# Mixing attention: the high and the low half of a head's values as one stationary tile

## The reference, cut to what matters

```python
z = jnp.einsum("bqhd,bkhd->bhqk", qb, kb) * scale
causal = s_idx < t_idx
log_beta = jax.nn.log_sigmoid(z)
log_fail = jnp.where(causal, log_beta - z, 0.0)
survive = lax.cumsum(log_fail, axis=3, reverse=True) - log_fail
a = jnp.where(causal, jnp.exp(log_beta + survive), 0.0)
o = jnp.einsum("bhqk,bkhd->bqhd", a, vb)
```

## Time and profile before

| | us |
|---|---|
| median of three runs | 2083.61 |
| lowest and highest run | 2078.96, 2084.55 |
| time of the profiled execution | 2086.71 |
| its span on the core | 2085.0 |
| outside the span | 1.7 |
| TensorE busy | 1934.9 (93%) |
| VectorE busy | 1078.7 (52%) |
| ScalarE busy | 854.9 (41%) |
| GpSimd busy | 199.7 (10%) |
| mean granted clock of TensorE, 1 is full | 0.937 |
| mixing stage, start to the end of `values(15)` | about 559 |

### The profile page before, as it was taken

How to read it: one execution, slowest core, us unless ns; L and a number is a source line. 1 busy time by engine, 2 the same in 40 slices (tenths; PEclk the granted TensorE clock), 3 DMA queues, 4 the chain that set the end, 5 groups by cost and what they waited for, 6 DMA issues and landing times. The chain is left out here.

```text
span 2085.0 us, 31580 instructions
## 1 busy us (share of the span) xinstructions
PE 1934.9 (93%) x12232; PEld 1686.0 (81%) x12232; DVE 1078.7 (52%) x1500; ACT 854.9 (41%) x1135; POOL 199.7 (10%) x329
## 2 busy tenths in 40 slices
PE   5999999999899988899999979699979999999996
PEld 5999999999899977799998857476757777778884
DVE  4434444433333324655542247999666776754543
ACT  4645555554422223333332224133346556543331
POOL 0100001000000000000000004777200000000000
PEclk8899999999899989999999989678889999999998
DMA  3121222122222233132233226311211212133331
GB/s 116 61 61 61 72 69 72 56 64 70 61 91 91 91 124 110 58 94 91 91 94 98 91 72 160 59 36 33 58 47 50 81 56 80 55 96 108 120 109 78
DMA packets 64501, 165.93 MB, mean 80 GB/s; under 512 B 21808, under 2 KB 21936, under 8 KB 64304
## 3 DMA queue, kind: packets, MB, share of 16 engines
q1 hardware_dynamic: 64432, 164.98, 25.9%
HBM read 154.20 MB, written 8.39 MB: 78 GB/s over the span
## 5 line engine op out<-in xcount | busy, mean ns | idle before, releaser
L1597 DVE TENSOR_TENSOR WL<-WR,WH 128x1024 fp32r<-128x1024 f32 x271 | 335.7, 1240 | 303.4 <-ACT WH L1169 294.2
L1169 ACT ACTIVATE WH<-WR 128x1024 fp32r<-128x1024 f32 x271 | 284.3, 1053 | 216.0 <-PE J L894 78.9
L702 PE MATMUL J<-XH,WH 128*128 128x264 f32 (+1 forms) x1376 | 295.0, 297 | 18.2 <-DVE XL L1601 18.0
L702 PE MATMUL J<-XL,WH 128*128 128x264 f32 (+1 forms) x1376 | 289.2, 293 | 0.0
L702 PE MATMUL J<-XH,WL 128*128 128x264 f32 (+1 forms) x1376 | 288.6, 292 | 0.0
L702 PEld LDWEIGHTS J<-XH,WH 128*128 128x128 f32 x1376 | 225.8, 199 | 23.6 <-issue 17.1
L702 PEld LDWEIGHTS J<-XL,WH 128*128 128x128 f32 x1376 | 224.3, 198 | 0.0
L702 PEld LDWEIGHTS J<-XH,WL 128*128 128x128 f32 x1376 | 223.4, 198 | 0.0
L2220 POOL TENSOR_SCALAR_AFFINE_SELECT E<-E 128x128 f32<-128x128 f32 (+1 forms) x160 | 45.0, 319 | 502.6 <-DVE E L1648 344.5
L923 PE MATMUL J<-X2H,WH 128*128 128x512 f32 x168 | 69.8, 416 | 8.8 <-DVE X2L L1878 8.8
L2242 POOL TENSOR_TENSOR SM<-SM 128x32 f32<-128x32 f32 x15 | 4.6, 309 | 728.3 <-DVEq L1912 727.2
(11 more groups left out here) (417 smaller groups left out, 4472.3 us busy)
## 6 DMA issues: line engine op xcount, KB each, us to landing
WR<-weights SPq DMA_DIRECT2D x271, 512.0 KB, 3.5
X<-tokens SPq DMA_DIRECT2D x4, 528.0 KB, 5.3
H<-tokens SPq DMA_DIRECT2D x1, 2112.0 KB, 8.2
res_dram<-H SPq DMA_DIRECT2D x1, 2048.0 KB, 8.1
u_dram<-UT SPq DMA_DIRECT2D x8, 256.0 KB, 2.2
US<-u_dram SPq DMA_DIRECT2D x16, 128.0 KB, 6.0
gate_dram<-GST SPq DMA_DIRECT2D x8, 256.0 KB, 2.2
GSB<-gate_dram SPq DMA_DIRECT2D x8, 256.0 KB, 3.6
```

The costliest lines, as they stand in the source:

```text
L702: mm = pe.matmul(o[:, 512 * h:512 * h + half], ws[:, s, w], xs[:, a:a + half], start=(k == 0 and i == 0), stop=(k == 7 and i == 2))
L1169: act.activation(WH[:, n % SPLIT, :], WR[:, n % RAW, :], ACT.Copy).then_inc(w_hi, 1)
L1597: dve.tensor_tensor(WL[:, n % SPLIT, :], WR[:, n % RAW, :], WH[:, n % SPLIT, :].bitcast(F32), ALU.subtract).then_inc(w_lo, 1)
```

## The change

The two tiles `VH` and `VL` become one, `VW`, with 64 high and 64 low columns of one head side by side. The stationary tile of a piece is now high | low of head h, 128 columns in all. Two passes, with `AH` and with `AL`, give the product with the high half in partitions 0 to 63 of the PSUM buffer and that with the low half in 64 to 127, the term of both low parts included. The two halves then have to be added: ScalarE copies the lower half (partitions 64 to 127) to a new tile `OT` in SBUF, VectorE adds the upper half to it there, and then ScalarE makes `OH` out of `OT` and VectorE `OL`. The PSUM buffer is freed after the addition.

Below stand the matmuls; then ScalarE's functions, its place in `mix` and its first copy of V; then VectorE's functions and first low part of V.

```diff
-                    for vs, ps in ((VH, AH), (VH, AL), (VL, AH)):
-                        mm = pe.matmul(o[:, at + a:at + b], vs[:, kt * P:(kt + 1) * P], ps[:, c + a:c + b],
+                    for ps in (AH, AL):
+                        mm = pe.matmul(o[:, at + a:at + b], VW[:, kt, h % 2].rearrange("p x d -> p (x d)"), ps[:, c + a:c + b],
...
+                act.wait_ge(o_sum, val(h + 1))
+                act.activation(OH[r, cols(m * L1, L1)], OT[r], ACT.Copy).then_inc(o_hi, 1)
+
+            def head_part(h, t):
...
                 act.wait_ge(pv_done, val(h + 1))
-                act.activation(halves(OH[r, cols(m * L1, L1)]), JV[as_lin(t) % 2][r], ACT.Copy).then_inc(o_hi, 1)
+                if positive(h):
+                    act.wait_ge(o_lo, val(h))
+                act.activation(halves(OT[r]), JV[as_lin(t) % 2][64:P], ACT.Copy).then_inc(o_part, 1)
...
                 if later:
-                    head_out(h - 1, m - 1, t + 2)
+                    head_part(h - 1, t + 2)
                 softplus(h)
                 split_hi(n + 5)
                 fail_hi(h)
+                if later:
+                    head_out(h - 1, m - 1, t + 2)
...
+                head_part(h, t + 9)
+                split_hi(n + 9)
                 head_out(h, m, t + 9)
-                split_hi(n + 9)
                 split_hi(n + 10)
...
-                act.activation(VH[:, 0:3 * P], J[(t + 5) % 2][:, 0:3 * P], ACT.Copy).then_inc(v_hi, 1)
+                act.activation(VW[:, 0:3, :, 0], heads(J[(t + 5) % 2][:, 0:3 * P]), ACT.Copy).then_inc(v_hi, 1)
...
-            def head_out(h, m, t):
+            def head_sum(h, t):
                 h, t = as_lin(h), as_lin(t)
                 r = slice(64 * (h % 2), 64 * (h % 2) + 64)
+                dve.wait_ge(o_part, val(h + 1))
+                dve.tensor_tensor(halves(OT[r]), JV[t % 2][0:64], halves(OT[r]), ALU.add).then_inc(o_sum, 1)
+                dve.wait_ge(o_sum, val(h + 1))
+                dve.nop().then_inc(read_out[t % 2], 1)
+
+            def head_lo(h, m):
...
                 dve.wait_ge(o_hi, val(h + 1))
-                low(halves(OL[r, cols(m * L1, L1)]), JV[t % 2][r], halves(OH[r, cols(m * L1, L1)]))\
-                    .then_inc(read_out[t % 2], 1)
+                low(OL[r, cols(m * L1, L1)], OT[r], OH[r, cols(m * L1, L1)]).then_inc(o_lo, 1)
...
-                low(VL[:, 0:3 * P], J[(t + 5) % 2][:, 0:3 * P], VH[:, 0:3 * P]).then_inc(read_out[(t + 5) % 2], 1)
+                low(VW[:, 0:3, :, 1], heads(J[(t + 5) % 2][:, 0:3 * P]), VW[:, 0:3, :, 0]).then_inc(read_out[(t + 5) % 2], 1)
```

More of the change, by code:

```diff
@@ L194, in halves, with heads @@
     return ap.rearrange("p (h t) -> p h t", h=2)
+def heads(ap):
+    return ap.rearrange("p (k x d) -> p k x d", x=2, d=64)
 def build(nc, weights, cond, params, tokens, bmat, cmat, positions, out):
@@ L236, in build @@
         QL = sb("QL", [P, L1], A1 + 2112, F32R)
-        VH = sb("VH", [P, 5 * P], A1 + 4224, F32R)
-        VL = sb("VL", [P, 5 * P], A1 + 6784, F32R)
+        VW = sb("VW", [P, 5, 2, 2, 64], A1 + 4224, F32R)
         assert A1 + 9344 <= U[8]
@@ L292, in build @@
         GST = sb("GST", [P, S2], M3 + 160)
-        assert M3 + 160 + 2048 <= 212800
+        OT = sb("OT", [P, L1], M3 + 160)
+        assert M3 + 160 + 2112 <= 212800
         M2H, M2L = tile2("M2H", 2), tile2("M2L", 5)
@@ L441, in build @@
         pv_done = sem("pv_done")
+        o_part = sem("o_part")
+        o_sum = sem("o_sum")
         o_hi = sem("o_hi")
+        o_lo = sem("o_lo")
         vt_done = sem("vt_done")
@@ L1244, in head_out @@
                 r = slice(64 * (h % 2), 64 * (h % 2) + 64)
+                act.wait_ge(o_sum, val(h + 1))
+                act.activation(OH[r, cols(m * L1, L1)], OT[r], ACT.Copy).then_inc(o_hi, 1)
+            def head_part(h, t):
+                h = as_lin(h)
+                r = slice(64 * (h % 2), 64 * (h % 2) + 64)
                 act.wait_ge(pv_done, val(h + 1))
-                act.activation(halves(OH[r, cols(m * L1, L1)]), JV[as_lin(t) % 2][r], ACT.Copy).then_inc(o_hi, 1)
+                if positive(h):
+                    act.wait_ge(o_lo, val(h))
+                act.activation(halves(OT[r]), JV[as_lin(t) % 2][64:P], ACT.Copy).then_inc(o_part, 1)
             def mix(m):
@@ L1275, in mix @@
                     act.wait_ge(pv_done, val(h))
-                act.activation(VH[:, 0:3 * P], J[(t + 5) % 2][:, 0:3 * P], ACT.Copy).then_inc(v_hi, 1)
+                act.activation(VW[:, 0:3, :, 0], heads(J[(t + 5) % 2][:, 0:3 * P]), ACT.Copy).then_inc(v_hi, 1)
                 weight_exp(h)
                 act.wait_ge(vt_done, val(2 * m + 2))
-                act.activation(VH[:, 3 * P:4 * P], J[(t + 6) % 2][:, 0:P], ACT.Copy)
-                act.activation(VH[0:META, 4 * P:], J[(t + 6) % 2][0:META, P:2 * P], ACT.Copy).then_inc(v_hi, 1)
+                act.activation(VW[:, 3:4, :, 0], heads(J[(t + 6) % 2][:, 0:P]), ACT.Copy)
+                act.activation(VW[0:META, 4:5, :, 0], heads(J[(t + 6) % 2][0:META, P:2 * P]), ACT.Copy).then_inc(v_hi, 1)
                 weight_hi(h)
@@ L1295, in _ @@
             repeat(act, DT, 1, mix)
+            head_part(HEADS - 1, T_MIX + 10 * DT)
             head_out(HEADS - 1, DT - 1, T_MIX + 10 * DT)
@@ L1604, in _ @@
             dve.memset(PP[:, 0:2], 0.0).then_inc(zeroed, 1)
-            dve.memset(VH[:, 4 * P:].bitcast(F32), 0.0)
-            dve.memset(VL[:, 4 * P:].bitcast(F32), 0.0).then_inc(zeroed, 1)
+            dve.memset(VW[:, 4].bitcast(F32), 0.0).then_inc(zeroed, 1)
             dve.wait_ge(w_hi, 1)
@@ L1678, in mix @@
                 if later:
-                    head_out(h - 1, m - 1, t + 2)
+                    head_sum(h - 1, t + 2)
                 else:
@@ L1684, in mix @@
                 fail_lo(h)
+                if later:
+                    head_lo(h - 1, m - 1)
                 split_lo(n + 6)
                 dve.wait_ge(v_hi, val(2 * m + 1))
-                low(VL[:, 0:3 * P], J[(t + 5) % 2][:, 0:3 * P], VH[:, 0:3 * P]).then_inc(read_out[(t + 5) % 2], 1)
+                low(VW[:, 0:3, :, 1], heads(J[(t + 5) % 2][:, 0:3 * P]), VW[:, 0:3, :, 0]).then_inc(read_out[(t + 5) % 2], 1)
                 dve.wait_ge(v_hi, val(2 * m + 2))
-                low(VL[:, 3 * P:4 * P], J[(t + 6) % 2][:, 0:P], VH[:, 3 * P:4 * P])
-                low(VL[0:META, 4 * P:], J[(t + 6) % 2][0:META, P:2 * P], VH[0:META, 4 * P:])\
+                low(VW[:, 3:4, :, 1], heads(J[(t + 6) % 2][:, 0:P]), VW[:, 3:4, :, 0])
+                low(VW[0:META, 4:5, :, 1], heads(J[(t + 6) % 2][0:META, P:2 * P]), VW[0:META, 4:5, :, 0])\
                     .then_inc(read_out[(t + 6) % 2], 1)
@@ L1709, in mix @@
                 low(YL[:, cols(m * L1, L1)], CT[:], YH[:, cols(m * L1, L1)]).then_inc(y_lo, 1)
-                head_out(h, m, t + 9)
+                head_sum(h, t + 9)
                 split_lo(n + 9)
@@ L1715, in mix @@
                 dve.tensor_copy(MROW[0:2, 0:2 * P], ZT[0:2, 0:2 * P]).then_inc(mod_rows, 1)
+                head_lo(h, m)
                 split_lo(n + 10)
@@ L1734, in _ @@
             repeat(dve, DT, 1, mix)
-            head_out(HEADS - 1, DT - 1, T_MIX + 10 * DT)
+            head_sum(HEADS - 1, T_MIX + 10 * DT)
+            head_lo(HEADS - 1, DT - 1)
             def gates(m):
```

## The result

| | before | changed |
|---|---|---|
| median of 8 runs, us | 2084.61 | 2092.49 |
| lowest and highest, us | 2075.17, 2091.17 | 2091.73, 2094.07 |
| profiled execution, span, us | 2085.0 | 2090.1 |
| mean granted clock | 0.937 | 0.934 |

The changed kernel is slower: the ratio of its runs to those of before is 1.004, 95% interval 1.0021 to 1.006. It does 144 matmuls less. A second series on another chip gave 1.0067 (1.0049 to 1.0085).

What follows compares the result with a forecast made beforehand. TensorE was taken to bound the mixing stage, busy 527 of 561 us. Matmuls gain 10.5 us, copies cost 0, the clock loses 18.6: +8.1 on the median of 2083.6, given as 2091; range 2072 to 2104.

Steps and rivals of the forecast that it cites:

- The matmuls: Values calls of the mixing stage: leaving out nine third passes saves 1.03 us a call; 10.5 us gained in all.
- The call behind the loop: Last values call, after the loop, at 1.2 GHz: a third of its 5.86 us is saved, taken as 2.0 us.
- An iteration at full clock: Loop iteration wholly at 2.4 GHz: 60.8 us forecast; more than 61 us would mean the copies are on the path.
- First heads gain nothing: Eight first-head values calls: in six iterations nothing is gained, as TensorE's wait for `LL` grows from 0.70 to 1.73 us.
- The two calls with cover behind them: First-head values calls in two iterations where TensorE came late itself: 0.68 us each to gain, 1.3 us together.
- The copies cost nothing: Added ScalarE and VectorE steps per head stand where those engines wait: 0 us taken, 20.8 us at most.
- The clock: Mixing loop: one more stretch at 1.2 GHz in each of seven iterations, 2.65 us each, 18.6 us lost.
- The nearest row: First iteration: TensorE idle 1.53 us, then scores; within 1.3 us the clock was at 1.2 GHz, for 6.8 us.
- thin parts nearer together: Second reason for more slow stretches: the same accumulates and scores, with fewer columns between; no size of its own.
- the rule from the Trainium skill: Names long waits for data as what costs the clock; by it a 1.7 us wait before accumulates costs nothing.
- The gain arrives: Rival: the clock falls as often as now, so the 10.5 us are gained: 2073 us, chance 0.30.
- The longer chain: Rival: added copies delay `LL` or `VT` in the mixing stage, 20.8 us at most: 2094 us, chance 0.05.

Runs made afterwards that it cites:

- the moved and filled one: Changed kernel with the second head's scores moved forward and 6 more matmuls at the head of the ada products: 2062.6 us, ratio 0.9893 against the kernel before.

## Why the prediction came out right, and which steps of it did not

**The matmuls: right.** 1.03 us a call was forecast, and 3.08 - 2.03 = 1.05 measured. The call behind the loop took 561.26 to 565.18, 3.92 us, where 5.86 less a third is 3.9.

```profile
561.26 0.56 PE L810 MATMUL J<-AH,VW 128*128 128x264 f32 x1 [4.99 <-DVE AL L1621]
...
565.18 0.51 PE L710 MATMUL J<-XH,WH 128*128 128x258 f32 x1
```

An iteration at full clock was forecast at 60.8 us. The first one of the loop took 62.57, with one stretch of 3.41 us at half clock and the first 0.7 us of another, which is 60.5 without them.

**First heads gain nothing: right.** 1.73 us of wait forecast, 1.77 measured. The two calls with cover behind them, worth 1.3 us, can't be found again, since in the changed kernel other iterations are the slow ones (one wait there is 0.25 us).

**The copies cost nothing: right, and closer than it looks.** The groups over the whole mixing stage, as rows 9 (busy us, mean ns, idle before):

```profile
L1684 DVE TENSOR_TENSOR OT<-J,OT 64x528 f32<-64x528 f32 x16 | 11.2, 697 | 14.7 <-ACT OT L1262 14.7
L1621 DVE TENSOR_TENSOR OL<-OT,OH 64x528 f32 x14 | 9.7, 696 | 0.2
L1262 ACT ACTIVATE OT<-J 64x528 f32<-64x528 f32 x16 | 9.7, 607 | 16.7 <-PE J L810 16.5
L1254 ACT ACTIVATE OH<-OT 64x528 f32 x14 | 9.0, 644 | 6.6 <-DVE OT L1684 6.5
```

The durations are those of the nearest rows to 0.05 us. The strided writes have none either: ScalarE's copy of 128x384 took 486 ns, 489 before. `VT` did come late, as rows 7 let one fear:

```profile
254.22 1.66 DVE L1621 TENSOR_TENSOR LL<-E,LH 128x1440 fp32r<-128x1440 f32 x1 [2.51 <-ACT LH L1234]
...
254.88 0.61 ACT L1285 ACTIVATE VT<-J 128x528 f32<-128x528 f32 x1
...
255.63 0.52 PE L821 MATMUL J<-IDENT,VT 128*128 128x128 f32 x3 [0.41 <-ACT VT L1285]
...
255.93 0.50 PE L791 MATMUL Z<-LH,NTRI 128*128 128x512 f32 x1
```

TensorE waited 0.41 us for it in three iterations, but `LL` ended at 255.88, so the accumulate could not have begun before 255.9 anyway. One wait has taken the place of another. The kernel without the copies agrees with it, against the first series of the changed kernel.

**The clock: the right term, with number and length mis-sized.** Forecast: seven more stretches, sixteen in all, near 80 us. Measured in the profiled execution: four more, thirteen in all, 81.5 us, each longer on average (6.3 in place of 4.8). By the forecast's own reckoning the loop lost 457.4 - 7 x 60.8 = 31.8 us to them, 2.4 us each, and 14.8 us more than before (17.0). 18.6 was forecast. So the net of the loop is +7.6 us, where it was forecast as -7.2 - 1.3 + 18.6 = +10.1. The term had the right sign and came within 4 us, with fewer and longer stretches than it was made of. That the median (2092.5) lies within 2 us of the forecast is in part luck: the second series of the same kernel has a ratio of 1.0067, some 14 us above the kernel before in place of 8.

**The reason given for the clock: half right.** The nearest row, the wait of 1.53 us in the first iteration, was the right one to go by. The second reason, thin parts nearer together, is refuted for second heads by the kernel that shortens these alone; for first heads it was not tried apart from the wait. And the rule from the Trainium skill (TensorE: Matmul & The Clock Gate, section "HAM oscillation — how this bites in real kernels"), by which a wait of 1.7 us would cost nothing, is not borne out here: the kernels with the wait of 1.8 us and those with it filled differ by 24 to 28 us, and the clock fell behind 23 of 38 such waits.

**The rivals.** The gain arrives (2073): this rival needed that the longer wait changes nothing, and that is wrong. Its number is reached, by 2069 to 2070, only when the wait is filled. The longer chain (2094) gave nearly the measured time by a wrong cause; the kernel without copies tells the two apart.

## What to carry to other kernels

Ask of every matmul that goes what TensorE waits for next. If that wait then grows in front of thin matmuls, as here from 0.7 to 1.8 us, the clock can take more than the matmuls gave. The cure is to start the chain that is waited for earlier, or even to fill the wait. Test the two sides of a symmetric change (here first and second heads) apart, since their sum hides that one gains 15 us and the other loses 11.

## What the runs showed of the hardware

- Between 0.9 and 1.8 us of idle time ahead of an accumulate the clock's cost goes from nothing measurable to 24 to 28 us over eight such waits. In the loop of the changed kernel the stretches at 1.2 GHz do not only become more. Some begin earlier, inside the thin matmuls, and last 13.7 us or more, in place of at most 6.8.
- Stretches at 1.2 GHz also come where TensorE did not wait. The kernel with 15 matmuls in the wait has ten of them in the loop, though in its profile it never waits there for `LL`.
- The spread of the runs differs much between kernels, and between series of one kernel: 2091.7 to 2094.1 and 2091.3 to 2102.6 for the two series of the changed kernel, 2086.7 to 2112.7 for the one that shortens first heads alone, 2059.2 to 2063.3 for the moved and filled one. What sets it was not tried.
- GpSimd's five masks take 1.18 us or 2.10 us. In the kernel with the moved scores they take 2.10, beside VectorE's split of weights, which starts just ahead of them; by these rows the 0.9 us between the two durations are more than the 0.65 us of wait that was left. In the changed kernel, at the same step, they take 1.18. That VectorE slows GpSimd here is inferred from the two rows and was not tried by itself.

With the scores moved:

```profile
268.95 1.66 DVE L1669 SCALAR_TENSOR_TENSOR E<-Z,E 128x1440 f32<-128x1440 f32 x1
270.52 1.22 DVE L1619 TENSOR_TENSOR WL<-WR,WH 128x1024 fp32r<-128x1024 f32 x1
270.68 2.10 POOL L2252 TENSOR_SCALAR_AFFINE_SELECT E<-E 128x128 f32<-128x128 f32 x5 [11.62 <-DVE E L1669]
```

In the changed kernel:

```profile
277.15 0.70 DVE L1733 TENSOR_TENSOR CT<-J,CV 128x528 f32<-128x528 f32 x1
277.30 1.18 POOL L2250 TENSOR_SCALAR_AFFINE_SELECT E<-E 128x128 f32<-128x128 f32 x5 [13.66 <-DVE E L1667]
```
